# RWKV chunk inverses in compact 32 by 32 tiles on four row groups, with one off-diagonal block as the last level

## The chip, the cores and the metric

One core of a Trainium2 chip runs the whole kernel. The metric is the device time of one execution in microseconds (us). Five engines work side by side and wait for each other through semaphores: TensorE (matmuls, PE in the profile; its weight loads are PEld), VectorE (DVE), ScalarE (ACT), GpSimd (POOL) and SyncE (SP). Matmuls write PSUM, of which there are 8 banks; GpSimd does not read it here.

## The reference, cut to what matters

Two blocks of a transformer-like model on 256 tokens of width 1024, batch 1: feed-forward layers, attention, an RWKV-7 time mixing in layer 1, then a second block with convolution, dense and expert layers. The change touches only the RWKV recurrence, 16 heads of width 64:

```python
def rwkv7_step(state, inp):
    r_t, w_t, k_t, v_t, a_t, b_t = inp
    sa = jnp.einsum('bhvk,bhk->bhv', state, a_t)
    state = (state * w_t[:, :, None, :] + sa[..., None] * b_t[:, :, None, :]
             + v_t[..., None] * k_t[:, :, None, :])
    return state, jnp.einsum('bhvk,bhk->bhv', state, r_t)
```

## The kernel before, in words

The kernel does the recurrence in chunks of 64 tokens (C), 4 chunks for 256 tokens. Within a chunk the steps form a triangular system: the inverse of a 64 by 64 unit triangular matrix is wanted for each head and chunk, Ti and its transpose TiT. Two heads lie in one tile of 128 partitions, a *pair* (kt, 0 to 7); a pair has 4 chunks times 2 heads = 8 such matrices. In a tile of 128 by 256, half of the partitions (c = 0 or 1) hold the even or the odd chunk, and N_MAT = 4 matrices stand side by side.

The inverse starts from blocks of 2 by 2 and doubles the block with each *level*: LEVELS = (2, 4, 8, 16, 32). A level is two steps. In the first ("x"), TensorE multiplies the matrix masked to this level's off-diagonal blocks (lev, made by GpSimd, line 2073) with half the columns of Ti, and ScalarE copies the product to X (line 1944). In the second ("t"), TensorE multiplies X with half the columns of TiT and TiT with X, and VectorE adds both products to TiT (line 2010) and Ti (line 2013). The last level forms only TiT's product. After it, for each of the 4 chunks in turn, the step U multiplies TiT with the right sides, and S and keys carry the state on (n = 12 and later).

Before level 0 stand two steps: the scores ("sc", 64 columns of keys against rates), masked by VectorE (line 1986), and the scores of keys against rates once more, both ways round ("ab"), from which VectorE makes the first Ti and TiT (lines 1993, 1996, 1997). With level 1's x comes the product Xs, with levels 2 and 3 a transpose each of BH and KH (line 1869).

`rwkv_tensor` interleaves this by an order written out by hand. There are 4 rounds (UNITS); a round works on two pairs at once, pair 0 in `weights_hi_scratch` and banks 0 and 1, pair 1 in `weights_lo_scratch` and banks 2 and 3. A round has 25 steps; in each, TensorE takes one step of pair 0, one of pair 1, and then 1 to 9 128x128 products of 256 columns of the next round's projections (DENSE_STEPS; LAST_STEPS with the output projection in round 4). The other engines run the same steps in the same order: `pair_scalar`, `pair_vector` (with `finish_vector` of the pair before in it, whose first operation is a reciprocal, line 2053) and `pair_gpsimd`. TensorE's queue is in order: a step of pair 0 that waits holds pair 1 and the dense products behind it.

All these products are in f32 and each shows as two records of LDWEIGHTS and MATMUL. A product of 64 rows and 64 columns of weights takes one of the four 64x64 tiles of the array, by the partitions that it reads and writes. All matmuls but the transposes have line 428, a helper.

Of the kernel before, what the change touches and what calls it, by code (L numbers as in the profile page):

```python
# [13 lines left out]
P = 128  # L14
# [35 lines left out]
N_RW_MASK = 10  # L50
# [28 lines left out]
def constant_arrays():  # L79
# [36 lines left out]
    rw = [row6 < col6, row6 <= col6]  # L116
    for b in (1,) + LEVELS:
        rw.append((row6 // (2 * b) == col6 // (2 * b)) & (row6 % (2 * b) < b) & (col6 % (2 * b) >= b))
    rw += [rw[2].T, row6 == col6]
    rw = np.tile(np.concatenate(rw, axis=1).astype(np.float32), (2, 1))  # L120
# [1160 lines left out]
class RwkvTiles:  # L1281
    def __init__(self, k):
        A = KT * T
        self.ld, self.r, self.kx, self.a = (k.arena[:, i * A:(i + 1) * A] for i in range(4))
        self.g = k.arena[:, 5 * A:6 * A]
        self.xx = self.bonus = k.arena[:, 6 * A:7 * A]
        self.VN = k.arena[:, 10 * A:11 * A]
        self.xm = {MIX_W: self.VN, MIX_A: self.g, MIX_K: k.arena[:, 7 * A:8 * A], MIX_G: self.VN,
                   MIX_R: k.arena[:, 8 * A:9 * A], MIX_V: k.arena[:, 4 * A:5 * A]}
        at = 9 * A  # L1290
        self.lora = k.arena[:, at:at + 4 * T]
        at += 4 * T
# [5 lines left out]
        self.masks = k.arena[:, ARENA - N_RW_MASK * RW_CHUNK:ARENA]  # L1298
# [476 lines left out]
class PairTiles:  # L1775
# [8 lines left out]
    def __init__(self, k, t, kt, slot):  # L1784
# [6 lines left out]
        self.Ti, self.TiT, self.U = (first[:, at + i * N_MAT * C:at + (i + 1) * N_MAT * C] for i in range(3))  # L1791
        self.lev = [second[:, i * N_MAT * C:(i + 1) * N_MAT * C] for i in range(2)]
        self.KH, self.BH, self.Xs, self.y, self.y2 = (second[:, (2 + i) * T:(3 + i) * T] for i in range(5))
        self.VN = blk(t.VN, kt)
        self.X = [k.sq[:, (slot * 4 + i) * N_MAT * C:(slot * 4 + i + 1) * N_MAT * C] for i in range(4)]
        self.X.append(k.hidden_scratch[:, slot * N_MAT * C:(slot + 1) * N_MAT * C])
# [7 lines left out]
    def mask(self, i, n=1):  # L1804
        return self.masks[:, i * C:(i + n) * C].rearrange("p (o t) -> p o t", o=1).to_broadcast([P, N_MAT, n * C])
# [6 lines left out]
def mat(z, c, m):  # L1812

    return z[part(c), m * C:(m + 1) * C]

# [5 lines left out]
def pair_tensor(k, t, kt, slot):  # L1821
# [21 lines left out]
    for s in range(TT):  # L1843
        for h, c in QUADRANTS:
            ins = mm(k, mat(z.b[h], 1 - c, 2 + s), z.bt[part(h), chunk_columns(s, c)],
                     z.ar[part(h), 0, chunk_columns(s, c)], True, True)
    ins.then_inc(*p.step((kt, "ab")))
    yield
    for li, size in enumerate(LEVELS):
        last = li == len(LEVELS) - 1  # L1850
        pe.wait_ge(*d.at((kt, "t", li - 1)))
        pe.wait_ge(*g.at((kt, "level", li)))
        lev, X = z.lev[li % 2], z.X[li]
        for m in range(N_MAT):
            for c in range(2):
                ins = mm(k, dense(b0[part(1 - c), m * C // 2:(m + 1) * C // 2], size), mat(lev, c, m),
                         half_columns(mat(z.Ti, c, m), size, 0), True, True)
        ins.then_inc(*p.step((kt, "x", li)))
        if li == 1:
            pe.wait_ge(*k.rw_act.at(("turn", kt // PAIRS)))  # L1860
            for m in range(N_MAT):
                for c in range(2):
                    ins = mm(k, mat(b1, 1 - c, m), z.MakT[part(c), m // 2 + m % 2 * 2, :], mat(z.VN, c, m), True, True)
# [13 lines left out]
        for m in range(N_MAT):  # L1877
            for c in range(2):
                ins = mm(k, dense(b1[part(c), m * C // 2:(m + 1) * C // 2], size), mat(X, c, m),
                         half_columns(mat(z.TiT, c, m), size, 1), True, True)  # L1880
            if not last:
                for c in range(2):
                    ins = mm(k, dense(b0[part(1 - c), m * C // 2:(m + 1) * C // 2], size), mat(z.TiT, c, m),
                             half_columns(mat(X, c, m), size, 0), True, True)
        ins.then_inc(*p.step((kt, "t", li)))
        yield
    for n in range(4):
        s, c = divmod(n, 2)
        if n > 0:
            pe.wait_ge(*(a.at((kt, "S", 1)) if n == 1 else d.at((kt, "S", n))))  # L1890
            for h in range(2):
                ins = mm(k, z.b[h][part(1 - c), P:P + HEAD], z.ar[part(h), 0, chunk_columns(s, c)], z.S[n][part(h), :],
                         True, True)
# [3 lines left out]
        else:  # L1897
            pe.wait_ge(*d.at((kt, "tt", len(LEVELS) - 1)))
        for h in range(2):
            ins = mm(k, b1[part(c), h * HEAD:(h + 1) * HEAD], mat(z.TiT, 1 - c, 2 * h + s), mat(z.Xs, 1 - c, 2 * s + h),  # L1900
# [33 lines left out]
def pair_scalar(k, t, kt, slot):  # L1934
# [7 lines left out]
    for li, size in enumerate(LEVELS):  # L1942
        act.wait_ge(*p.at((kt, "x", li)))
        act.copy(half_columns(z.X[li], size, 0), dense(b0[:, 0:N_MAT * C // 2], size)).then_inc(*a.step((kt, "X", li)))
# [29 lines left out]
def pair_vector(k, t, kt, slot):  # L1974
# [8 lines left out]
    for h in range(2):  # L1983
# [3 lines left out]
                          z.b[h][:, :].rearrange("p (m x) -> p m x", m=N_MAT), z.mask(0, 2), ALU.mult)\  # L1987
# [3 lines left out]
    for h in range(2):  # L1991
        for to, at, mask in ((z.Ti, 0, 8), (z.TiT, P, 2)):
            dve.tensor_tensor(mats(to)[:, 2 * h:2 * h + 2, :], z.b[h][:, at:at + P].rearrange("p (m t) -> p m t", m=2),
                              z.mask(mask)[:, 0:2, :], ALU.mult).then_inc(*d.step((kt, "T0", h, mask)))
    dve.wait_ge(*d.at((kt, "T0", 1, 2)))
    dve.tensor_tensor(mats(z.Ti), mats(z.Ti), z.mask(9), ALU.add).then_inc(*d.step((kt, "t", -1)))
    dve.tensor_tensor(mats(z.TiT), mats(z.TiT), z.mask(9), ALU.add).then_inc(*d.step((kt, "TiT")))
    yield
    earlier = finish_vector(k, t, kt - PAIRS, slot) if kt >= PAIRS else None
    for li, size in enumerate(LEVELS):  # L2000
# [8 lines left out]
        piece = half_columns(z.TiT, size, 1)  # L2009
        dve.tensor_tensor(piece, piece, dense(b1[:, 0:N_MAT * C // 2], size), ALU.add).then_inc(*d.step((kt, "tt", li)))  # L2010
        if not last:
            piece = half_columns(z.Ti, size, 0)
            dve.tensor_tensor(piece, piece, dense(b0[:, 0:N_MAT * C // 2], size), ALU.add)\
                .then_inc(*d.step((kt, "t", li)))
        yield
    for n in range(4):
        s, c = divmod(n, 2)
        if n > 0:
# [3 lines left out]
            for h in range(2):  # L2022
                piece = mat(z.Xs, 1 - c, 2 * s + h)
                ins = dve.tensor_tensor(piece, z.b[h][part(1 - c), P:P + HEAD], piece, ALU.add)
# [43 lines left out]
def pair_gpsimd(k, t, kt, slot):  # L2068
# [3 lines left out]
    def level(li):  # L2072
        pool.tensor_tensor(mats(z.lev[li % 2]), z.MabT, z.mask(3 + li), ALU.mult).then_inc(*g.step((kt, "level", li)))
# [6 lines left out]
    pool.wait_ge(*d.at((kt, "sc", 1)))  # L2080
# [3 lines left out]
    pool.wait_ge(*p.at((kt, "ab")))  # L2084
# [3 lines left out]
    for li in range(len(LEVELS) - 2):  # L2088
        pool.wait_ge(*p.at((kt, "x", li)))
        level(li + 2)  # L2090
        yield

# [1137 lines left out]
```

## Time and profile before

| | |
|---|---|
| time, median of 3 runs | 2735.32 us (2733.24 to 2735.78) |
| the profiled execution | 2738.52 us, span 2737.0 us, mean granted TensorE clock 0.985 |
| busy over the span: TensorE, its weight loads, VectorE, ScalarE, GpSimd | 96%, 84%, 76%, 59%, 8% |
| the four RWKV rounds | 785 to about 1010 us of the span |

The span runs from the first to the last instruction; the time of the execution is 1.5 us more. Matmuls are pipelined and their ends are modelled, so a busy TensorE need not be one at its peak, and the starts of its records tell more than their lengths. A granted clock of 1.00 is 2.4 GHz, 0.50 is 1.2 GHz.

### The profile page before, as it was taken

The page shows a single profiled execution, that of the slowest core. Times are in us where ns is not written, and L with a number is a line of the kernel's source. Part 1 is how long each engine was busy: PE and PEld are TensorE (multiplying, and loading weights), DVE is VectorE, ACT ScalarE, POOL GpSimd, SP SyncE. Part 2 cuts the span into 40 slices and gives each one's busy share as a digit, 9 for nine tenths or more (in the row PEclk, how much of TensorE's full clock was granted, in tenths as well). Part 3 has the DMA queues.
Part 4 walks back from the last instruction along what each step waited for, and adds up shares of the span by engine and source line. Part 5 has one row for each costly group of instructions (what it writes and reads, how often), then busy time and mean ns, then how long its engine had stood idle before and what let it go on. Part 6 is the DMA issues. An engine that isn't in the chain of part 4 may idle for free.

```text
span 2737.0 us, 43598 instructions
## 1 busy us (share of the span) xinstructions
PE 2635.5 (96%) x17668; PEld 2290.9 (84%) x17668; DVE 2068.2 (76%) x2973; ACT 1614.9 (59%) x2394; POOL 226.1 (8%) x229
## 2 busy tenths in 40 slices
PE   8999899999899999999999898999999999999997
PEld 7989789899787779998899896888888888888886
DVE  6667776776744557668655686999999999999995
ACT  5556455555332235543555535877787778778785
POOL 1102000000011117011600010000000000000000
PEclk9999999999999999999999999999999999999999
DMA  7553245455331125543355433999999999899992
GB/s 272 185 185 110 106 169 185 172 183 185 113 106 67 66 92 185 185 166 116 135 186 185 145 130 122 378 351 349 352 375 351 349 351 366 335 364 363 352 375 82
DMA packets 84605, 604.91 MB, mean 221 GB/s; under 512 B 9400, under 2 KB 9528, under 8 KB 12016
## 3 DMA queue, kind: packets, MB, share of 16 engines
q1 hardware_dynamic: 82016, 594.05, 58.9%
q10 hardware_dynamic: 2032, 4.85, 0.5%
q8 instruction: 144, 2.36, 0.4%
q0 software_dynamic: 352, 3.15, 0.3%
q14 instruction: 61, 0.50, 0.1%
HBM read 600.96 MB, written 1.05 MB: 220 GB/s over the span
## 4 chain that ended last, share of the span: by engine, by line
PE 88%; DVE 9%; ACT 2%; issue 1%; DMA 1%; ACTq 0%; DVEq 0%
PE bank L428 86%; DVE arena L2266 2%; DVE weights_lo L418 2%; PE bank L2856 1%; DVE arena L1200 1%; ACT weights_hi L410 1%; DVE rstd L479 1%; DMA x_T<-in_x 0%; DVE x_T L734 0%; DVE arena L2289 0%; DVE arena L555 0%; DVE arena L1202 0%; ACT x_T L546 0%; DVE arena L2980 0%; PE bank L1869 0%
## 5 line engine op out<-in xcount | busy, mean ns | idle before, releaser
L418 DVE TENSOR_TENSOR weights_lo<-raw_weights,weights_hi 128x1024 fp32r<-128x1024 f32 x816 | 1004.1, 1249 | 389.5 <-ACT weights_hi L410 383.9
L410 ACT CAST weights_hi<-raw_weights 128x1024 fp32r<-128x1024 f32 x816 | 849.5, 1050 | 333.4 <-PE bank L428 319.1
L428 PE MATMUL bank<-source,weights_hi 128*128 128x512 f32 (+1 forms) x3040 | 876.7, 356 | 43.0 <-DVE weights_lo L418 18.2
L428 PE MATMUL bank<-source,weights_lo 128*128 128x256 f32 x2400 | 682.2, 284 | 0.0
L428 PEld LDWEIGHTS bank<-source,weights_hi 128*128 128x128 f32 x3040 | 541.8, 194 | 130.6 <-issue 28.0
L428 PEld LDWEIGHTS bank<-source,weights_lo 128*128 128x128 f32 x2400 | 463.2, 193 | 0.1
L418 DVE TENSOR_TENSOR weights_lo<-arena,weights_hi 128x1024 fp32r<-128x1024 f32 x278 | 336.5, 1225 | 32.0 <-ACT weights_hi L410 28.5
L410 ACT CAST weights_hi<-arena 128x1024 fp32r<-128x1024 f32 x278 | 292.2, 1053 | 56.5 <-PE bank L428 40.3
L428 PE MATMUL bank<-weights_hi,source 128*128 128x512 f32 (+1 forms) x1024 | 309.6, 386 | 3.4 <-issue 2.8
L428 PE MATMUL bank<-hidden_hi,weights_hi 128*128 128x256 f32 x912 | 258.3, 283 | 0.0
L428 PE MATMUL bank<-hidden_lo,weights_hi 128*128 128x256 f32 x912 | 258.1, 283 | 0.0
L428 PE MATMUL bank<-hidden_hi,weights_lo 128*128 128x256 f32 x912 | 257.9, 283 | 0.0
L428 PEld LDWEIGHTS bank<-weights_hi,source 128*128 128x128 f32 x1024 | 186.3, 191 | 36.7 <-issue 4.1
L428 PE MATMUL bank<-weights_lo,source 128*128 128x512 f32 (+1 forms) x512 | 195.0, 381 | 0.0
L428 PE MATMUL bank<-weights_hi,hidden_hi 128*128 128x512 f32 x448 | 174.9, 390 | 6.2 <-issue 4.1
L428 PE MATMUL bank<-weights_hi,other_source_hi 128*128 128x512 f32 x448 | 179.7, 401 | 0.0
L428 PEld LDWEIGHTS bank<-hidden_hi,weights_hi 128*128 128x128 f32 x912 | 174.7, 192 | 2.6
L428 PE MATMUL bank<-weights_lo,other_source_hi 128*128 128x512 f32 x448 | 175.2, 391 | 0.0
L428 PEld LDWEIGHTS bank<-hidden_hi,weights_lo 128*128 128x128 f32 x912 | 174.9, 192 | 0.0
L428 PEld LDWEIGHTS bank<-hidden_lo,weights_hi 128*128 128x128 f32 x912 | 174.8, 192 | 0.1
L428 PE MATMUL bank<-weights_hi,other_source_lo 128*128 128x512 f32 x448 | 174.7, 390 | 0.0
L428 PE MATMUL bank<-weights_lo,hidden_hi 128*128 128x512 f32 x448 | 174.4, 389 | 0.0
(317 smaller groups left out, 3387.0 us busy)
## 6 DMA issues: line engine op xcount, KB each, us to landing
raw_weights<-in_exp_in SPq DMA_DIRECT2D x134, 1024.0 KB, 5.4
arena<-in_exp_in SPq DMA_DIRECT2D x90, 1024.0 KB, 5.4
raw_weights<-in_exp_w SPq DMA_DIRECT2D x67, 1024.0 KB, 5.3
arena<-in_exp_w SPq DMA_DIRECT2D x45, 1024.0 KB, 5.6
raw_weights<-in_ffn_w_down SPq DMA_DIRECT2D x44, 1024.0 KB, 5.0
raw_weights<-in_ffn_w_up SPq DMA_DIRECT2D x43, 1024.0 KB, 5.0
raw_weights<-in_ffn_w_gate SPq DMA_DIRECT2D x42, 1024.0 KB, 4.9
raw_weights<-in_dense_w SPq DMA_DIRECT2D x33, 1024.0 KB, 4.9
```

The costliest lines, as they stand in the source:

```text
L410: k.act.copy(k.weights(j)[0], raw_half(k, j)).then_inc(k.w_hi_ready, 1)
L418: k.dve.tensor_tensor(lo, raw_half(k, j), hi.bitcast(F32), ALU.subtract).then_inc(k.w_ready, 1)
L428: return k.pe.matmul(dst, lhsT, rhs, start=start, stop=stop, skip_group_check=shared)
L479: k.dve.reciprocal(k.rstd[:, :], k.std[:, :]).then_inc(*k.normed.step((f, "rstd")))
L1200: k.dve.reciprocal(s_r, s_s).then_inc(*k.at_dve.step(("root", u)))
L2266: ins = k.dve.scalar_tensor_tensor(y, tap, w, y, ALU.mult, ALU.add)
L2856: ins = k.pe.transpose(bank[:, i * P:(i + 1) * P], k.act_buf[:, n % 2 * T + i * P:n % 2 * T + (i + 1) * P], ident)
```

## The change

Up to blocks of 32, Ti, TiT, the level masks and X are kept as 32 by 32 blocks: of each 64 by 64 matrix only the two diagonal blocks (b = 0, 1). Partitions 32 (2c + b) and on hold block b of chunk parity c, and the tiles are 128 by 128 where they were 128 by 256. The products of levels 0 to 3 are then 32 by 32, each on the diagonal tile of one of four row groups, with 16 streamed columns where there were 32, and twice as many. The ab step gives the blocks directly: 32 columns of weights, 32 streamed, twice as many products. The last level is one block: the masked product (`MabT`) of rows 0 to 31 and columns 32 to 63 with Ti's first block, copied by ScalarE to X32, times TiT's second block; VectorE copies the result to its place in `full`, a 64 by 64 form of TiT, whose diagonal blocks GpSimd copies from TiT once level 3 is done. U reads `full`. VectorE first copies the ab scores to M, from which GpSimd makes the level masks (before: from MabT) and VectorE the first TiT. Xs and the state products keep their chunk's partition half, where they wrote the other. The masks are smaller. The core of the diff, VectorE's and GpSimd's parts after TensorE's:

```diff
-    for s in range(TT):
-        for h, c in QUADRANTS:
-            if s == 0 and c == h:
-                pe.wait_ge(*d.at((kt, "sc", h)))
-            mm(k, mat(z.b[h], c, s), z.ar[part(h), 0, chunk_columns(s, c)], z.bt[part(h), chunk_columns(s, c)],
-               True, True)
...
+    for turned in range(2):
+        for s in range(TT):
+            for b in range(2):
+                for h, c in QUADRANTS:
...
+                    keys, rates = z.bt[part(h), block_columns(s, c, b)], z.ar[part(h), 0, block_columns(s, c, b)]
+                    lhsT, rhs = (keys, rates) if turned else (rates, keys)
+                    ins = mm(k, tile32(z.b[h], c, b, 2 * turned + s), lhsT, rhs, True, True)
...
+        if last:
+            for m in range(N_MAT):
+                for c in range(2):
+                    ins = mm(k, tile32(b0, c, 1, m), z.MabT[rows32(c, 0), m, BLOCK:C], tile32(z.Ti, c, 0, m), True, True)
+        else:
...
+            for m in range(N_MAT):
+                for c in range(2):
+                    for b in range(2):
+                        ins = mm(k, half_tile(b0, c, b, m, size), tile32(lev, c, b, m),
+                                 half_columns(tile32(z.Ti, c, b, m), size, 0), True, True)
...
         for m in range(N_MAT):
+            if last:
+                for c in range(2):
+                    ins = mm(k, tile32(b1, c, 0, m), tile32(z.X32, c, 1, m), tile32(z.TiT, c, 1, m), True, True)
+                continue
             for c in range(2):
-                ins = mm(k, dense(b1[part(c), m * C // 2:(m + 1) * C // 2], size), mat(X, c, m),
-                         half_columns(mat(z.TiT, c, m), size, 1), True, True)
-            if not last:
-                for c in range(2):
-                    ins = mm(k, dense(b0[part(1 - c), m * C // 2:(m + 1) * C // 2], size), mat(z.TiT, c, m),
-                             half_columns(mat(X, c, m), size, 0), True, True)
+                for b in range(2):
+                    ins = mm(k, half_tile(b1, c, b, m, size), tile32(X, c, b, m),
+                             half_columns(tile32(z.TiT, c, b, m), size, 1), True, True)
+            for c in range(2):
+                for b in range(2):
+                    ins = mm(k, half_tile(b0, c, b, m, size), tile32(z.TiT, c, b, m),
+                             half_columns(tile32(X, c, b, m), size, 0), True, True)
...
             pe.wait_ge(*d.at((kt, "tt", len(LEVELS) - 1)))
+            pe.wait_ge(*g.at((kt, "full")))
...
     for h in range(2):
-        for to, at, mask in ((z.Ti, 0, 8), (z.TiT, P, 2)):
-            dve.tensor_tensor(mats(to)[:, 2 * h:2 * h + 2, :], z.b[h][:, at:at + P].rearrange("p (m t) -> p m t", m=2),
-                              z.mask(mask)[:, 0:2, :], ALU.mult).then_inc(*d.step((kt, "T0", h, mask)))
-    dve.wait_ge(*d.at((kt, "T0", 1, 2)))
-    dve.tensor_tensor(mats(z.Ti), mats(z.Ti), z.mask(9), ALU.add).then_inc(*d.step((kt, "t", -1)))
-    dve.tensor_tensor(mats(z.TiT), mats(z.TiT), z.mask(9), ALU.add).then_inc(*d.step((kt, "TiT")))
+        ins = dve.tensor_copy(z.M[:, 2 * h * BLOCK:2 * (h + 1) * BLOCK], z.b[h][:, 2 * BLOCK:4 * BLOCK])
+    ins.then_inc(*d.step((kt, "M")))
+    for h in range(2):
+        dve.tensor_tensor(mats(z.Ti)[:, 2 * h:2 * h + 2, :],
+                          z.b[h][:, 0:2 * BLOCK].rearrange("p (m t) -> p m t", m=2),
+                          z.mask(5, 2), ALU.mult).then_inc(*d.step((kt, "T0", h)))
+    dve.wait_ge(*d.at((kt, "M")))
+    dve.tensor_tensor(mats(z.TiT), mats(z.M), z.mask(0), ALU.mult).then_inc(*d.step((kt, "TiT0")))
+    dve.wait_ge(*d.at((kt, "TiT0")))
+    dve.tensor_tensor(mats(z.Ti), mats(z.Ti), z.mask(6), ALU.add).then_inc(*d.step((kt, "t", -1)))
+    dve.tensor_tensor(mats(z.TiT), mats(z.TiT), z.mask(6), ALU.add).then_inc(*d.step((kt, "TiT")))
...
+    pool.wait_ge(*d.at((kt, "tt", len(LEVELS) - 2)))
+    for c in range(2):
+        for b in range(2):
+            ins = pool.tensor_copy(mats(z.full)[rows32(c, b), :, b * BLOCK:(b + 1) * BLOCK], mats(z.TiT)[rows32(c, b), :, :])
+    ins.then_inc(*g.step((kt, "full")))
```

The helpers that it calls:

```python
def rows32(c, b):
    return slice((2 * c + b) * BLOCK, (2 * c + b + 1) * BLOCK)

def tile32(z, c, b, m):
    return z[rows32(c, b), m * BLOCK:(m + 1) * BLOCK]

def half_tile(bank, c, b, m, size):
    return dense(bank[rows32(c, b), m * BLOCK // 2:(m + 1) * BLOCK // 2], size)
```

## Rows read from the trace of the kernel before

**Rows 1.** The page, part 4: the chain that ended last, by engine and by line.

```profile
...
PE 88%; DVE 9%; ACT 2%; issue 1%; DMA 1%; ACTq 0%; DVEq 0%
PE bank L428 86%; DVE arena L2266 2%; DVE weights_lo L418 2%; PE bank L2856 1%; DVE arena L1200 1%; ACT weights_hi L410 1%; DVE rstd L479 1%; DMA x_T<-in_x 0%; DVE x_T L734 0%; DVE arena L2289 0%; DVE arena L555 0%; DVE arena L1202 0%; ACT x_T L546 0%; DVE arena L2980 0%; PE bank L1869 0%
...
```

**Rows 2.** Busy time by stretch: us from:to, its length, then busy us (instructions) by engine.

```profile
...
785.00:954.00 169.00, 167.73 (x2888) 133.59 (x2892) 80.40 (x239) 39.31 (x118) 29.93 (x42) 1.00 0.18 64
954.00:1010.00 56.00, 54.46 (x912) 42.68 (x904) 27.53 (x73) 10.72 (x35) 10.12 (x14) 0.91 0.20 77
785.00:1010.00 225.00, 222.20 (x3788) 176.27 (x3789) 107.93 (x312) 50.03 (x152) 40.05 (x56) 0.98 0.19 68
...
```

**Rows 3.** The waits between 785 and 1010 us: total us, times, longest.

```profile
...
PEld bank L428 <- DVE weights_lo_scratch L1996: 1.6, 1, 1.6
...
PE bank L428 <- DVE weights_hi_scratch L2013: 1.1, 2, 0.5
...
```

**Rows 4.** Timeline, TensorE, round 1: start us, us until the last ends, what, xrecords.

```profile
...
789.03 1.16 PE L428 MATMUL bank<-arena 64*64 64x64 f32 x64
790.12 1.13 PE L428 MATMUL bank<-normed_T,consts 128*128 128x256 f32 x4
...
791.52 1.46 PE L428 MATMUL bank<-arena,raw_weights 128*128 128x256 f32 x6
792.91 0.66 PE L428 MATMUL bank<-weights_hi_scratch 64*64 64x32 f32 x16
793.56 0.66 PE L428 MATMUL bank<-weights_lo_scratch 64*64 64x32 f32 x16
...
795.20 0.25 PE L428 MATMUL bank<-weights_hi_scratch,squares 64*64 64x32 f32 x2
795.22 0.25 PE L428 MATMUL bank<-squares,weights_hi_scratch 64*64 64x32 f32 x2
795.28 0.23 PE L428 MATMUL bank<-weights_hi_scratch,squares 64*64 64x32 f32 x2
...
795.69 0.23 PE L428 MATMUL bank<-weights_lo_scratch,squares 64*64 64x32 f32 x2
...
```

**Rows 5.** Timeline, TensorE, round 1: a product with 2 streamed columns.

```profile
...
823.62 1.05 PE L428 MATMUL bank<-consts,normed_T 128*128 128x2 f32 x8
824.54 0.68 PE L428 MATMUL bank<-arena,raw_weights 128*128 128x256 f32 x2
```

**Rows 6.** Timeline, VectorE, round 3: both pairs, from the first mask.

```profile
...
904.03 0.88 DVE L1993 TENSOR_TENSOR weights_hi_scratch<-bank,arena 128x128 f32<-128x128 f32 x4 [0.85 <-PE bank L428]
...
907.65 0.41 DVE L1997 TENSOR_TENSOR weights_lo_scratch<-weights_lo_scratch,arena 128x256 f32<-128x256 f32 x1
...
```

**Rows 7.** Groups by form, the rounds: busy us, mean ns of one, idle before.

```profile
...
L2024 DVE TENSOR_TENSOR weights_hi_scratch<-bank,weights_hi_scratch 64x64 f32<-64x64 f32 x24 | 4.2, 215 | 22.9 <-PE bank L428 22.9
...
L2073 POOL TENSOR_TENSOR weights_hi_scratch<-weights_hi_scratch,arena 128x256 f32<-128x256 f32 x20 | 15.3, 766 | 200.9 <-DVE weights_hi_scratch L1986 174.7 <-PE bank L428 26.2
...
L2351 POOL MEMSET arena<- 128x64 f32 x6 | 0.6, 150 | 179.4 <-DVE x_T L2439 179.4
...
```

**Rows 8.** Timeline, TensorE, round 3, levels 0 and 1.

```profile
...
907.78 0.66 PE L428 MATMUL bank<-weights_lo_scratch 64*64 64x32 f32 x16
...
911.72 0.66 PE L428 MATMUL bank<-weights_hi_scratch 64*64 64x32 f32 x16 [0.54 <-DVE weights_hi_scratch L2013]
...
913.74 1.13 PE L428 MATMUL bank<-arena,raw_weights 128*128 128x256 f32 x4
...
```

**Rows 9.** Timeline, TensorE, round 4, levels 0 and 1.

```profile
...
961.16 1.01 PE L428 MATMUL bank<-weights_lo_scratch 64*64 64x32 f32 x16 [1.54 <-DVE weights_lo_scratch L1996]
...
970.73 1.49 PE L428 MATMUL bank<-arena,raw_weights 128*128 128x256 f32 x4
...
```

**Rows 10.** Timeline, VectorE and TensorE, round 4: level 3, first U.

```profile
...
982.29 0.29 DVE L2010 TENSOR_TENSOR weights_lo_scratch<-weights_lo_scratch,bank 128x128 f32<-128x128 f32 x1
...
986.57 0.44 PE L428 MATMUL bank<-weights_hi_scratch 64*64 64x64 f32 x4
...
```

More of the change, by code:

```diff
@@ L49 @@
 LEVELS = (2, 4, 8, 16, 32)
-N_RW_MASK = 10
+BLOCK = 32
+N_SMALL_MASK = 7
+RW_MASKS = 2 * RW_CHUNK + N_SMALL_MASK * BLOCK
 PARAMS = [
@@ L115, in constant_arrays @@
     row6, col6 = row[0:RW_CHUNK], col[:, 0:RW_CHUNK]
[L116 to L120, printed above, removed]
+    wide = np.tile(np.concatenate([row6 < col6, row6 <= col6], axis=1).astype(np.float32), (P // RW_CHUNK, 1))
+    row3, col3 = row[0:BLOCK], col[:, 0:BLOCK]
+    small = []
+    for b in (1,) + LEVELS[:-1]:
+        small.append((row3 // (2 * b) == col3 // (2 * b)) & (row3 % (2 * b) < b) & (col3 % (2 * b) >= b))
+    small += [small[0].T, row3 == col3]
+    rw = np.concatenate([wide, np.tile(np.concatenate(small, axis=1).astype(np.float32), (P // BLOCK, 1))], axis=1)
     t = np.arange(T)
@@ L1851, in pair_tensor @@
         pe.wait_ge(*d.at((kt, "t", li - 1)))
-        pe.wait_ge(*g.at((kt, "level", li)))
-        lev, X = z.lev[li % 2], z.X[li]
-        for m in range(N_MAT):
-            for c in range(2):
-                ins = mm(k, dense(b0[part(1 - c), m * C // 2:(m + 1) * C // 2], size), mat(lev, c, m),
-                         half_columns(mat(z.Ti, c, m), size, 0), True, True)
+        if last:
[3 more added lines that the diff above has]
+        else:
+            pe.wait_ge(*g.at((kt, "level", li)))
+            lev, X = z.lev[li % 2], z.X[li]
+            for m in range(N_MAT):
[3 more added lines that the diff above has]
+                                 half_columns(tile32(z.Ti, c, b, m), size, 0), True, True)
         ins.then_inc(*p.step((kt, "x", li)))
@@ L1943, in pair_scalar @@
         act.wait_ge(*p.at((kt, "x", li)))
-        act.copy(half_columns(z.X[li], size, 0), dense(b0[:, 0:N_MAT * C // 2], size)).then_inc(*a.step((kt, "X", li)))
+        if li == len(LEVELS) - 1:
+            ins = act.copy(z.X32, b0[:, 0:N_MAT * BLOCK])
+        else:
+            ins = act.copy(half_columns(z.X[li], size, 0), dense(b0[:, 0:N_MAT * BLOCK // 2], size))
+        ins.then_inc(*a.step((kt, "X", li)))
         if 0 < li < 4:
@@ L2008, in pair_vector @@
             dve.wait_ge(*d.at((kt, "TiT")))
-        piece = half_columns(z.TiT, size, 1)
-        dve.tensor_tensor(piece, piece, dense(b1[:, 0:N_MAT * C // 2], size), ALU.add).then_inc(*d.step((kt, "tt", li)))
-        if not last:
+        if last:
+            for c in range(2):
+                ins = dve.tensor_copy(mats(z.full)[rows32(c, 0), :, BLOCK:C],
+                                      b1[rows32(c, 0), 0:N_MAT * BLOCK].rearrange("p (m t) -> p m t", m=N_MAT))
+            ins.then_inc(*d.step((kt, "tt", li)))
+        else:
+            piece = half_columns(z.TiT, size, 1)
+            dve.tensor_tensor(piece, piece, dense(b1[:, 0:N_MAT * BLOCK // 2], size), ALU.add)\
+                .then_inc(*d.step((kt, "tt", li)))
             piece = half_columns(z.Ti, size, 0)
-            dve.tensor_tensor(piece, piece, dense(b0[:, 0:N_MAT * C // 2], size), ALU.add)\
+            dve.tensor_tensor(piece, piece, dense(b0[:, 0:N_MAT * BLOCK // 2], size), ALU.add)\
                 .then_inc(*d.step((kt, "t", li)))
@@ L2072, in level @@
     def level(li):
-        pool.tensor_tensor(mats(z.lev[li % 2]), z.MabT, z.mask(3 + li), ALU.mult).then_inc(*g.step((kt, "level", li)))
+        pool.tensor_tensor(mats(z.lev[li % 2]), mats(z.M), z.mask(1 + li), ALU.mult).then_inc(*g.step((kt, "level", li)))
     def hat(src, name):
@@ L2087, in pair_gpsimd @@
     hat(z.kt_, "KH")
-    for li in range(len(LEVELS) - 2):
+    for li in range(len(LEVELS) - 3):
         pool.wait_ge(*p.at((kt, "x", li)))
```

45 lines of the change are left out of this document (25 added, 20 removed).

## The prediction

> **What bounds the kernel now.** I read the page first: the chain that ended last is 88% TensorE, 86% of it line 428, which every matmul shares [rows 1]. The change touches only the four RWKV rounds, 785 to 1010 us, so I asked for those windows next: TensorE is busy 222.20 of 225 us, VectorE 107.93, ScalarE 50.03, GpSimd 40.05 [rows 2]. A busy TensorE may only be pipelined, so two checks. The waits list gives it few waits on other engines: 1.6 us once for line 1996, 1.1 us in two waits for line 2013 [rows 3]. And the timeline shows matmul groups starting back to back [rows 4]. So TensorE's own spacing of matmuls sets the time here; a nanosecond off it comes off the span, except where it merely reaches a wait sooner.
>
> **The unit: a slot.** A product in f32 is two records. Records on one tile of the array follow each other in fixed slots; different tiles run side by side. In the t products of level 0, records of four 64x64 tiles start together (795.20, 795.22), the next four from 795.28, and pair 1's begin at 795.69: seven groups in 0.41 us, so 58.4 ns a slot, 0.49 us for the 8 slots of a pair with the longer first one (80 ns) [rows 4]. 64 columns streamed cost no more: 64 such records take 1.09 us to the next group, 16 slots again. The stream is thus not what fills the slot. With 128 columns of weights and 2 streamed columns a record takes 0.92/8 = 115 ns, its first one long as well [rows 5]. Half the weight columns, half the slot: loading the weights sets it, 50 to 57 ns per 64 columns. For 32 columns I extrapolate (58.4 - 50/2) to (58.4 - 57/2) = 30 to 33 and take 32 ns. Bounds: 29 ns (half of 58.4) and 58.4 (it does not shrink).
> On this price alone a page can be asked: the Trainium skill, "TensorE: Matmul & The Clock Gate", section LDWEIGHTS, has the load cost its columns at 1.2 GHz whatever the rows, 27 ns for 32. By it, as an estimate, the slots below would come to 120 x 27 = 3.2 us a pair; no trace here has a 32-column load.
>
> **Slots per pair (8 pairs).** Now: the second group of scores ("ab", 32 records on 4 tiles) 8; X products of levels 0 to 3 (16 records on 2 tiles) 8 each; their t products (32 on 4) 8 each; the last level's two phases 8 each: 8 + 32 + 32 + 16 = 88 x 58.4 = 5.14 us. After: ab has 64 records on 8 tiles, 8 slots; X has 32 records on the 4 diagonal tiles, 8; t has 64 on the same 4, 16; the last level is 8 products in each of two phases, on 2 tiles, 8 and 8: 8 + 32 + 64 + 16 = 120 x 32 = 3.84 us. Eight pairs: **-10.4 us**. The break-even slot is 5140/120 = 42.8 ns; the bounds give -13.3 (29 ns) and +15.0 (58.4).
>
> **Tile size switches.** Six 128-row records start at 791.52 and the next 64x64 group at 792.91: 1.39 us where 6 x 0.216 is 1.30. Back again, 789.03 to 790.12 is 1.09 where 16 slots are 0.94 to the last start plus 0.06 [rows 4]. A change of tile size costs 0.09 us each way. Most steps keep their count, since dense work already stands between them. New is level 1: X (32x32), Xs (64x64), X, Xs adds 3 switches a round, 12 in all, 1.1 us, and 0.3 for the long first slots behind them: **+1.4 us**. No row has 32x32 against 64x64; bounds 0 and, at twice the price, 2.8.
>
> **VectorE at a round's start.** Before TensorE's second X group, VectorE masks four PSUM pieces per pair (0.22 us apart) and makes two 128x256 products with masks: 904.03 to 908.06 for both pairs, 4.0 us [rows 6]. After: two copies and two masks of half the width from PSUM, one mask and two adds at 128x128. A 64x64 PSUM operation still takes 0.215 [rows 7], so little is saved on each: 4 x 0.18 + 3 x 0.25 = 1.46 a pair, 2.9 for both, 1.1 less; with ab ending 0.2 earlier for pair 0, VectorE is 1.3 ahead. What waits on it:
> - Rounds 1 to 3, pair 1's first X: 793.56 comes 0.65 after 792.91 where 0.49 is enough. **-0.15 x 3**, gone.
> - Rounds 2 and 3, level 1: TensorE idle 0.54 before 911.72 behind line 2013 [rows 8]. TensorE comes 0.9 sooner (0.42 ab, 0.42 X, 0.15, less 0.09 t), VectorE 1.4: 0.5 of the 0.54 goes. **-0.47 x 2**. The two reciprocals of the previous pairs, 3.3 us between, stay and are late next.
> - Round 4, pair 1's first X: idle 1.54 before 961.16 [rows 9]. VectorE 1.06 sooner for that operand, TensorE 0.63: **-0.43**.
> Together -1.8; bounds 0 and -3.3, all of these waits.
>
> **Costed at nothing.** ScalarE's copies of X halve in width and have 1.0 us of dense work behind them. GpSimd's level masks go from 128x256 (0.77 us) to 128x128, one fewer per pair; level 0's now waits for the VectorE copy M, the first thing VectorE does after ab, and has over 2 us until its X. The mask load is smaller. New on GpSimd: four copies per pair of the diagonal blocks into the full matrix, behind level 3's VectorE add (line 2010, 982.29), before U (986.57, pair 1's 0.29 later) [rows 10]. GpSimd does nothing else then; behind them in its queue stands only the next round. With the last level 0.84 shorter, 8 copies have 3.7 us. Bounds for one: 0.15 (memset 128x64) and 0.77 (128x256 product) [rows 7]; at 0.3 they take 2.4 and hide; at 0.77 pair 1's U waits 2.5 a round. After the rounds, TensorE goes straight on into the output projection, and the DMA engines are busy 0.20 of round 4 [rows 2], so the gain is not given back to a transfer.
>
> **Sum.** -10.4 + 1.4 - 1.8 = -10.8 us. The profiled execution took 2738.5 (span 2737.0), 3.2 above the median of 2735.3. In it the granted clock fell from 2.4 to 1.2 GHz in round 4 right behind the 1.54 us idle. From pair 1's first X to the dense work behind Xs took 9.57 us there (961.16 to 970.73) against 5.95 in round 3 (907.78 to 913.74) [rows 8, 9]: 3.6 us, about what the profile lies above the median. So 2735.3 - 10.8 = 2724.5, or, if the shorter idle spares the fall, 2738.5 - 10.8 - 3.6 = 2724.1. I say **2724**.
>
> **A rule against it.** Four tiles' records start within 0.02 us and 32 of them within 0.49 us, 15 ns each [rows 4]. The change adds 112 products a pair, 1792 records in all, each streaming only 16 columns. The Trainium skill, "TensorEngine Tiling (Array Packing)", section Instruction Overhead, holds that every matmul carries some 60 cycles however few its columns, and advises against taking tiles from a dimension already small. Were that a price for the whole engine (25 ns), the added records alone would cost an estimated +45 us; the rows refute this, as a floor per tile it lies under my 32 ns.
>
> **Rivals.**
> 1. *The small records cost the same slot or arrive no faster.* 58.4 ns for 32 columns gives +15.0 + 1.4 - 1.8 = +14.6, **2750**. The same sign if the engine takes one record per 15 ns, the densest long run seen: t and ab then need 64 x 15 = 0.96 against 0.49, +0.47 x 40 = +18.8, less 0.4: 2754. It is slower from a mean slot of about 43 ns. For: no 32-column load in the trace, nothing denser than 15 ns for long. Against: 115 to 58 on halving the columns, and groups of four within 0.02 us.
> 2. *A slot half way*, about 40 ns: 120 x 40 = 4.8, -2.7 - 0.4 = -3.1, **2732**.
> 3. *The clock.* Smaller tiles occupy less of the array; round 4 shows the clock fall after idling, the first three rounds hold 1.00 [rows 2]. If every round's levels fell, 4 x 3.6 = 14.4 on top of -10.8: +3.6, **2739**. Against: dense work at full width stands in every step.
> 4. *The full matrix comes late*: 2.5 us in rounds 2 to 4 (round 1 has more dense work there), 7.5, **2732**.
>
> **Chances and range.** Forecast 68% (2718 to 2730, by a slot of 29 to 35 ns, switches of nothing to 1.4, waits of 0 to -3.3), rival 1 13%, rival 2 8%, rival 3 6%, rival 4 5%. One measurement tells 0.2%, 5.5 us. Faster: the forecast and about half of rivals 2 and 4, 0.74; slower: rival 1 and half of rival 3, 0.17; the rest 0.09. The range, 2717 to 2741, takes in all but rival 1 and scraps.
>
> **What would show it.** In the profile after: LDWEIGHTS of 32 columns with starts on one tile 32 ns apart; t of a pair in 0.51 us (now 0.49), X in 0.27; 12 more switches of 0.09; line 428's records up by 1792; no wait of TensorE for GpSimd's copies; the rounds some 11 us shorter and the clock at 1.00 in rounds 1 to 3. A t phase near 1 us, or TensorE waiting for the full matrix, would prove me wrong.

## The result, and the profile after

2793.5 us, the median of 4 runs (2784.0 to 2804.3), against 2734.3 before (also 4 runs now): ratio **1.0215 [1.0189, 1.0242]**, 59 us slower. The forecast was 2724, with a range of 2717 to 2741. The profiled execution took 2788.6 (span 2787.0), 50.1 more than that of before, and the whole of it lies in the rounds: TensorE's first score record to the first product behind the rounds now takes 285.6 us, where it took 234.2.

The page after: TensorE's count, what released the chain, and the queue that brings instructions.

```profile
span 2787.0 us, 47222 instructions
PE 2673.1 (96%) x19460; PEld 2314.3 (83%) x19460; DVE 2066.4 (74%) x2989; ACT 1613.1 (58%) x2394; POOL 218.3 (8%) x253
...
q8 instruction: 158, 2.59, 0.4%
...
PE 88%; DVE 8%; ACT 2%; issue 1%; DMA 1%; ACTq 0%; DVEq 0%
```

The records are up by 1792 (17668 before), as forecast. The instruction queue has 14 packets more than before's 144: 1792 loads and 1792 matmuls are 14 times 256 instructions. The chain of waits looks as in [rows 1]; its shares tell nothing. The stretches tell it; columns as in [rows 2]. Rounds 1 to 4, each cut where the levels end, then all of it:

```profile
786.77:827.80 41.03, 38.30 (x1139) 30.20 (x1139) 11.68 (x41) 7.52 (x22) 8.73 (x20) 0.83 0.14 54
827.80:854.75 26.95, 26.95 (x290) 21.20 (x286) 11.33 (x38) 5.95 (x19) 0.00 (x0) 1.00 0.23 79
854.75:893.15 38.40, 35.09 (x1115) 26.99 (x1114) 17.15 (x50) 6.56 (x20) 8.19 (x20) 0.75 0.17 59
893.15:926.70 33.55, 33.55 (x282) 25.19 (x278) 11.21 (x37) 5.53 (x18) 0.00 (x0) 0.72 0.08 32
926.70:963.80 37.10, 34.74 (x1116) 26.78 (x1115) 17.02 (x49) 6.55 (x20) 8.19 (x20) 0.77 0.17 61
963.80:989.27 25.47, 25.43 (x283) 19.75 (x279) 11.42 (x38) 5.50 (x18) 0.00 (x0) 1.00 0.12 43
989.27:1028.20 38.93, 31.20 (x1105) 24.15 (x1104) 15.23 (x44) 5.55 (x18) 8.22 (x20) 0.82 0.29 112
1028.20:1072.30 44.10, 42.80 (x308) 31.93 (x304) 19.12 (x47) 12.20 (x28) 0.00 (x0) 0.73 0.13 47
786.77:1072.30 285.53, 268.06 (x5616) 206.19 (x5616) 114.16 (x341) 55.37 (x163) 33.33 (x80) 0.81 0.17 61
```

Two things are new. First, the granted clock: 0.81 over the rounds, where [rows 2] had 0.98. The same steps, of rounds 2 and 3, took 33.55 us at 0.72 and 25.47 at 1.00. A granted clock of 0.72 means that 56% of the stretch, 18.8 us, ran at 1.2 GHz, and these cost 8.1 us: **0.43 us for each us at 1.2 GHz**. Second, TensorE is idle: busy 31.20 of 38.93 us in round 4's levels. Its waits in the rounds (us in all, times, longest), beside [rows 3]:

```profile
PE bank L432 <- issue: 12.1, 13, 2.5
PE bank L1903 <- issue: 3.0, 2, 1.5
...
PE bank L432 <- DVE weights_lo_scratch L2045: 1.1, 1, 1.1
```

"issue" is a wait for nothing that the profile shows: **15.1 us in 15 holes**, of which the rounds had none before. They open in the middle of a step's products. Three that follow each other in round 4 (timeline), and the records between them (stretches):

```profile
1015.79 0.20 PE L432 MATMUL bank<-weights_lo_scratch,squares 32*32 32x16 f32 x2 [0.35 <-issue]
1019.75 0.44 PE L1903 MATMUL bank<-consts,arena 128*128 128x128 f32 x2 [1.54 <-issue]
1023.42 0.25 PE L432 MATMUL bank<-squares,weights_lo_scratch 32*32 32x16 f32 x7 [1.20 <-issue]
```

```profile
1015.80:1019.70 3.90, 2.41 (x127) 1.75 (x127) 1.02 (x4) 0.80 (x3) 0.00 (x0) 1.00 0.02 4
1019.70:1023.40 3.70, 2.48 (x127) 2.00 (x127) 0.35 (x2) 0.37 (x1) 1.14 (x4) 1.00 0.02 4
```

127 loads, 127 matmuls and two waits are 256 instructions, one packet of 16 KB of the instruction queue, and the holes are 3.7 and 4.0 us apart at full clock. The other holes of the rounds stand whole multiples of 256 instructions apart too, to one instruction, with TensorE's waits counted in. My reading: TensorE's program comes in instruction pages of 256, and the next one was not there.

### The profile page after: what moved, and what is told of

It reads as the page before. It is cut to its first block, busy times and chain, and to the rows that moved or that the text cites. A ratio compares the mean times of both kernels' runs of the same rounds, so it can differ in the third digit from the quotient of the medians.

```text
span 2787.0 us, 47222 instructions
## 1 busy us (share of the span) xinstructions
PE 2673.1 (96%) x19460; PEld 2314.3 (83%) x19460; DVE 2066.4 (74%) x2989; ACT 1613.1 (58%) x2394; POOL 218.3 (8%) x253
## 4 chain that ended last, share of the span: by engine, by line
PE 88%; DVE 8%; ACT 2%; issue 1%; DMA 1%; ACTq 0%; DVEq 0%
PE bank L432 86%; DVE arena L2326 2%; DVE weights_lo L422 2%; PE bank L2916 1%; DVE arena L1204 1%; ACT weights_hi L414 1%; DVE rstd L483 1%; PE bank L1903 0%; DMA x_T<-in_x 0%; DVE x_T L738 0%; DVE arena L2349 0%; DVE arena L559 0%; DVE arena L1206 0%; ACT x_T L550 0%; DVE arena L3040 0%
## 5 line engine op out<-in xcount | busy, mean ns | idle before, releaser
L432 PE MATMUL bank<-arena,raw_weights 128*128 128x256 f32 (+2 forms) x624 | 185.2, 439 | 8.7 <-DVE arena L1699 8.7
```

The costliest lines, as they stand in the source:

```text
L432: return k.pe.matmul(dst, lhsT, rhs, start=start, stop=stop, skip_group_check=shared)
```

## The experiments

Medians, each beside before's on the same chip, and the ratio with its 95% interval; "rounds" is the length of the rounds in the profiled execution, with its clock there, "issue" the sum of TensorE's waits of that name in the rounds (for supply alone, in the added products).

The recorded texts below name three explanations. Theory A: the program is supplied too slowly, which makes the holes, and the holes let the clock fall. Rival B: there is no such limit, and the holes belong to the 32x32 tiles. Rival C: small tiles lower the clock by themselves.

| kernel | us | before | ratio | rounds, clock | issue |
|---|---|---|---|---|---|
| after | 2793.5 | 2734.3 | 1.0215 [1.0189, 1.0242] | 285.6, 0.81 | 15.1 |
| 64x64 products doubled | 2760.8 | 2736.3 | 1.0103 [1.0085, 1.0120] | 258.9, 0.99 | 5.6 |
| half of the products | 2747.9 | 2736.3 | 1.0042 [1.0009, 1.0075] | 244.0, 0.90 | 0.4 |
| more dense work | 2772.7 | 2736.3 | 1.0135 [1.0119, 1.0152] | 272.7, 0.99 | 6.5 |
| last block alone | 2732.6 | 2736.3 | 0.9982 [0.9971, 0.9993] | 230.0, 0.99 | 0 |
| supply alone | 2825.7 | 2736.5 | one run | | 29.2 |
| dense work earlier | 2786.7 | 2736.5 | 1.0189 [1.0173, 1.0204] | 284.5, 0.84 | 17.0 |
| half, round 4 covered | 2745.8 | 2736.5 | 1.0042 [1.0027, 1.0057] | 223.9, 0.99 | 0 |
| last block, round 4 covered | 2729.3 | 2736.5 | 0.9975 [0.9963, 0.9987] | 227.8, 1.00 | 0 |
| small filler | 2839.4 | 2733.4 | 1.0388 [1.0365, 1.0412] | 327.1, 0.75 | 5.7 |
| idle | 2845.0 | 2733.4 | 1.0397 [1.0370, 1.0424] | 341.1, 0.71 | 33.6 |
| cover alone | 2733.3 | 2733.4 | 0.9997 [0.9986, 1.0007] | 230.2, 1.00 | 0 |
| half the idle | 2771.1 | 2735.3 | 1.0117 [1.0073, 1.0161] | 275.5, 0.87 | 14.0 |

**Supply alone.**

```diff
+    for i in range(1024):
+        r = slice(i % 4 * 32, i % 4 * 32 + 32)
+        mm(k, k.bank[0][r, 0:16], ident[r, 0:32], ident[r, 0:16], True, True)
+    for i in range(512):
+        r, q = slice(i % 2 * 64, i % 2 * 64 + 64), slice(i // 2 % 2 * 64, i // 2 % 2 * 64 + 64)
+        mm(k, k.bank[i % 2][q, 0:16], ident[r, 0:64], ident[r, 0:16], True, True)
     for p in range(UNITS):
```

> The kernel before with 1024 products of 32x32 on four diagonal tiles (2048 records) and 512 of 64x64 on the four 64x64 tiles (1024 records) in a row ahead of the first round, with operands in SBUF and no waits. Theory A (the program comes in pages of 256 instructions, one per 3.4 to 4 us when none is in stock): after the stock is used up both sections run at the same pace of 27 to 31 ns a record, whatever the tile: 55 to 64 us for the first section (16 pages), 27 to 32 us for the second (8 pages); holes end at multiples of 256 instructions; the whole 2817 to 2831. Rival B (no limit of supply; the tiles' own pace of 8 ns a record for 32x32, 14.6 ns for 64x64): 17 and 15 us, no holes, 2767.

A stretch of the first section, and the instruction queue in it (packets, MB, share):

```profile
785.50:837.70 52.20, 26.60 (x1792) 25.10 (x1793) 0.00 (x0) 0.00 (x0) 0.00 (x0) 0.50 0.02 6
```

```profile
q8 instruction: 14, 0.23, 1.8%
```

```profile
785.50 1.90 PE L428 MATMUL bank<-consts 32*32 32x16 f32 x128 [2.51 <-issue]
788.96 1.90 PE L428 MATMUL bank<-consts 32*32 32x16 f32 x128 [1.55 <-issue]
```

128 records run in 1.9 us, then TensorE stands; 1792 records and 14 packets in 52.2 us, **3.73 us for 256 instructions, 29.1 ns a record**, with no work on the other engines. The whole section is at 1.2 GHz (clock 0.50), and yet the pace is that of the changed kernel's holes at full clock, 3.7 to 4.0 us. A limit of supply by itself is thus shown, and 2825.7, a single run, lies in its range. The 64x64 section ran at 28.8 ns, but at 1.2 GHz its own pace is about that (two times 14.6), so it tells nothing. In the section "Instruction fetch mechanics" of the page "Runtime: NRT & Kernel Launch", the Trainium skill has the same blocks of 256 instructions, fetched one while another runs; it holds that the fetch is hidden behind the issue of instructions. The blocks agree with the 256 between holes; the hiding does not hold here, and the measurement decides.

**64x64 products doubled.**

```diff
-            for c in range(2):
+            for c in (0, 1) if last else (0, 1, 0, 1):
                 ins = mm(k, dense(b1[part(c), m * C // 2:(m + 1) * C // 2], size), mat(X, c, m),
...
+                if li != 1:
+                    mm(k, dense(b1[part(c), m * C // 2:(m + 1) * C // 2], size), mat(lev, c, m),
+                       half_columns(mat(z.Ti, c, m), size, 0), True, True)
```

> The kernel before with its 64x64 products doubled, until its levels issue as many matmul records as the changed kernel's (112 more products a pair but for 8, 104): each ab product and each t product of levels 0 to 3 is issued twice, and each X product of levels 0, 2, 3 and 4 once more on one of the two idle tiles. By slots of 58.4 ns the added work costs 8 slots in 32 t steps and 8 in 8 ab steps, 15.0 + 3.7 = +18.7 us, and nothing for X: 2753. Theory A (TensorE's program arrives in pages of 16 KB, 256 instructions, and no faster than one in 3.4 to 4 us; the levels of the changed kernel use them up faster): holes in the middle of groups at 256-instruction boundaries here as well, 10 to 20 us in all, 2763 to 2775, more if the clock falls behind them. Rival B (the holes are a matter of the 32x32 tiles): no holes, 2753. Rival C (the clock falls because tiles are small, not because of holes): granted clock of the rounds 0.98 as before, whether or not there are holes.

```profile
PE bank L428 <- issue: 5.6, 8, 1.8
```

Holes without a single 32x32 tile: rival B falls. They are 5.6 us, less than the 10 to 20 expected (2753 + 5.6 is 2759, measured 2760.8). That the doubled work takes longer and so leaves the supply more time is my explanation, not tried. The clock held (0.99), as rival C had it: 5.6 us of holes among 64x64 products, twice as many as before, did not lower it.

**Half of the products.**

```diff
-                    for b in range(2):
+                    for b in range(1):
                         ins = mm(k, half_tile(b0, c, b, m, size), tile32(lev, c, b, m),
```

> The changed kernel with the products of the second diagonal block (b = 1) left out in ab and in the X and t steps of levels 0 to 3: as few instructions as before, 8 slots for X and 16 for t on each tile that still works, half of the tiles idle. What is left out makes the result another one; the time is what counts. By slots the time is the changed kernel's forecast, 2724. Theory A: no holes, and since the holes' idle lets the clock fall, a clock near 0.98 in the rounds, 2720 to 2732. Rival B (32x32 tiles make the holes): holes stay, 2740 or more. Rival C (small tiles lower the clock by themselves): no holes, but a granted clock of 0.85 or less in the rounds, 2750 to 2775.

Its rounds 2 and 4:

```profile
841.17:893.32 52.15, 51.41 (x945) 40.27 (x944) 28.40 (x86) 12.01 (x38) 8.62 (x20) 1.00 0.19 63
...
946.10:1027.10 81.00, 78.52 (x961) 59.00 (x960) 34.09 (x91) 17.70 (x46) 8.28 (x20) 0.68 0.20 77
```

As many instructions as before, and the holes are gone (0.4 us of issue in all). Round 2 takes 52.15 us, where it took 53.96 before: with a clock of 1.00 and no holes, these small products, half as many, save time. But the clock fell without holes: 0.90 in the rounds, median 2748, between the ranges of theory A and of rival C and nearer C's. Theory A's second half, that the holes make it fall, is refuted in this form. The clock fell behind round 4's wait for VectorE, so I took that for the trigger.

**Half, with round 4's wait covered.**

```diff
-LAST_STEPS = [2, 2] + [2, 1] * 5 + [1] * 10 + [2, 2, 1]
+LAST_STEPS = [2, 4] + [2, 1] * 5 + [1] * 10 + [1, 1, 1]
```

> The changed kernel with the products of the second diagonal block left out as before (its output is another one), and in round 4 two dense products moved from the last steps to behind ab, where TensorE idled for VectorE and the clock fell for 51 us (2747). If the idle starts the fall and the small work only keeps the clock from coming back: no fall in round 4 in most runs, clock 0.985 or more, 2718 to 2726. If small tiles lower the clock by themselves: the fall stays, at 0.975 to 0.98, 2742 to 2748.

2745.8, as without it: the first branch is wrong, and the time and the clock (0.974 to 0.980 in all runs but one) are those of the second, small tiles by themselves. The profiled run, 2722.6, is the exception: no fall in round 4 and rounds of 223.9 us, 10.4 less than before; the other seven took 2739 to 2756. The idle of round 4 was not what decides.

**More dense work, and the same filler on a small tile.**

```diff
         pe.wait_ge(*d.at((kt, "t", li - 1)))
+        if li > 0:
+            mm(k, b1[:, 2 * P:4 * P], ident, k.const[:, 0:2 * P], True, True)
...
+        mm(k, b0[:, 2 * P:4 * P], ident, k.const[:, 0:2 * P], True, True)
```

> The changed kernel with one more 128x128 product of 256 columns (constants times constants, into columns that nobody reads) ahead of the small products of each X step from level 1 on and of each t step: 9 a pair, 72 in all, 2 records of 0.216 us each, and for the second pair of a round two tile size switches of 0.09: +38 us by its own work. If holes and the fallen clock are what the change costs, the denser work thins out the instructions per us and keeps the clock up: 2724 + 38 = 2762, so faster than the changed kernel's 2793 by some 30 us although it does more; granted clock of the rounds 0.95 or more, holes under 8 us. If both have another cause (a wait, the products themselves): 2793 + 38 = 2831.

In the second kernel these products read `ident[0:32, 0:32]` and `k.const[0:32, 0:2 * P]`.

> The changed kernel with the same 72 additional products as in the run with more dense work, but on one 32x32 tile instead of the whole array (32 rows and 32 columns of weights, 256 streamed columns, the same 0.216 us a record, no tile size switch): 72 x 0.43 = 31 us of TensorE time that thins out the instructions as before but leaves the array nearly empty. If the holes alone let the clock fall (theory A): holes as few as there (4 to 6 us), clock 0.985, 2724 + 4 + 31 + 5 = 2764. If work on few rows and columns lowers the clock by itself (rival C): the same few holes, but a clock of 0.965 or less, 2785 to 2815.

With 128x128 filler:

```profile
786.73:1059.41 272.68, 264.35 (x5760) 203.89 (x5761) 114.25 (x341) 55.09 (x164) 33.09 (x80) 0.99 0.18 63
...
PE bank L432 <- issue: 6.5, 5, 2.7
```

With 32x32 filler:

```profile
785.69:1112.76 327.07, 319.73 (x5761) 231.73 (x5761) 114.44 (x341) 55.33 (x164) 32.78 (x80) 0.75 0.15 52
...
PE bank L432 <- issue: 5.7, 8, 1.9
```

The changed kernel with 72 products more is **21 us faster** than without them. Both fillers take as many instructions and leave as few holes (6.5 and 5.7 us); only how much of the array they fill differs. With full width the clock is 0.99, with 32 by 32 it is 0.75, and 67 us lie between them. Neither time was forecast well: 2772.7 for 2762, and 2839.4 is 24 us above even rival C's range. The kernel with the small filler was at 1.2 GHz for 54.6 us on end in round 2. The 3.0 us before, and that stretch:

```profile
869.90:872.90 3.00, 2.77 (x113) 1.97 (x106) 2.48 (x8) 0.18 (x1) 0.36 (x2) 1.00 0.03 5
872.90:927.50 54.60, 54.60 (x791) 36.09 (x788) 9.49 (x39) 6.51 (x23) 3.07 (x10) 0.50 0.07 22
```

TensorE had been busy for 2.77 of 3.00 us. Narrow work lowers the clock with hardly any idle, and no more than its twin has: rival C is right in this.

**Idle in the kernel before**, and half as much.

```diff
         for m in range(N_MAT):
+            if m == 2 and not last and kt % PAIRS == 0:
+                for _ in range(48):
+                    pe.wait_ge(*k.rw_pre_dve.at(("ops", kt // PAIRS)))
```

> The kernel before with idle time in the middle of pair 0's t step in levels 0 to 3 of each round: a row of waits that are long met, 24 or more of 51 ns each, 1.2 us or more, 16 times: about as much idle as the holes of the changed kernel, in the same steps, but with 64x64 tiles. If idle of this size in the levels lets the clock fall (theory A): the time grows by the idle (20 us) and by a fallen clock, 0.975 or less, 2775 or more. If the tiles decide (rival C): clock 0.98 to 0.987, 2735 + 20 = 2755.

```profile
786.99:1128.04 341.05, 304.59 (x3825) 234.86 (x3825) 116.33 (x325) 57.01 (x164) 39.57 (x56) 0.71 0.14 50
```

> The kernel before with half the row of met waits in the same 16 places: by the run with the whole row (48 waits, holes of 2.3 us) holes of 1.2 us, 18 to 19 us in all, which is the sum of the holes of the changed kernel, on 64x64 tiles. If idle alone of this size is what lowers the changed kernel's clock: clock 0.965 to 0.970, 2735 + 18.5 + some 35 = 2785 to 2795. If the narrow tiles have to come with it: clock 0.98 or more, 2752 to 2762. Between them, both count.

```profile
787.53:1063.07 275.54, 258.65 (x3825) 202.14 (x3825) 115.92 (x325) 56.99 (x164) 39.52 (x56) 0.87 0.18 62
...
PE bank L428 <- issue: 14.0, 16, 1.1
```

The first idle came out larger than meant, 33.6 us; with it the clock fell to 0.71 on unchanged 64x64 tiles. The second gave 14.0 us of the 18.5 expected, about the changed kernel's holes: two of four runs took 2758 to 2760 (clock of the whole run 0.98) and two 2782 (0.97). So idle alone lowers the clock too, and narrow tiles do; the changed kernel has both. At its median this kernel loses 36 us, 14 as idle and some 22 by the clock, where the changed kernel loses 42 by the clock (worked out below): an estimate of the share that idle alone has, and a rough one, since the four runs fall into two groups.

**Dense work earlier.** (LAST_STEPS likewise, for round 4.)

```diff
-DENSE_STEPS = [4, 5] + [2, 1] * 5 + [2] * 10 + [3, 3, 2]
+DENSE_STEPS = [4, 5] + [2, 2] * 5 + [2, 1] * 5 + [3, 3, 2]
```

> The changed kernel with 5 of each round's dense products moved from the later steps into the level steps, nothing added: rounds 1 to 3 [2, 2] instead of [2, 1] a level and [2, 1] instead of [2, 2] behind them, round 4 likewise. Theory A: five levels get 2.1 us more cover, so holes shrink by about as much a round (some 6 of the 15 us), and the levels are denser in 128-row work, so the clock falls less often: 2765 to 2785. If only waits of the later steps come of it: 2793 to 2800.

Missed: 2786.7, just above the range; issue is 17.0 us, not less, and the clock 0.84 for 0.81. Five products a round, moved, are too few; the 18 above, added, held the clock and left 6.5 us of issue.

**The parts that could stay.** The last level alone (its first phase; the rest of the edit is the change's):

```diff
+        if last:
+            for m in range(N_MAT):
+                for c in range(2):
+                    ins = mm(k, b0[rows32(1 - c, 1), m * 32:(m + 1) * 32], z.MabT[rows32(c, 0), m, 32:C],
+                             half_of(z.Ti, c, 0, m, 0), True, True)
```

> The kernel before with one part of the change alone: the last level as one off-diagonal block of 32x32 products in the old 64x64 layout, with ScalarE's copy of it in compact form, two VectorE copies of 32x128 in the place of one 128x128 add, and no GpSimd mask for that level. As many records as before. By slots: 16 of 58.4 ns become 16 of 32 ns a pair, 0.42 us, 8 pairs: -3.4 us; VectorE's second copy may take 0.15 of it back a round. All theories: no new holes, 2731 (2729 to 2734). Rival C, that small products lower the clock by themselves, would show a clock fall behind level 4 in most rounds and 2735 to 2745.

with the covered wait of round 4 (the edit of LAST_STEPS above):

> The kernel before with the last level as one block of 32x32 products, and in round 4 two dense products moved from the last steps to behind ab, ahead of pair 1's first X, where TensorE is idle for 1.54 us. The block gives -3.4 (2731); the cover takes 0.86 of the idle, and if that idle is what starts the fall of the clock in round 4, the 3.6 us of the fall go too: 2727 (2725 to 2729). If the clock falls all the same: 2730 to 2731.

and that cover alone:

> The kernel before with the moved dense products of round 4 alone (two of them from the last steps to behind ab), to split the 7 us that this and the last block gained together: block 3.4 by slots, so 3.6 from the cover, of which 0.86 is the idle and the rest the clock: 2731 to 2733. If the gain was the block's alone: 2735 to 2736.

The block gave 3.7 us for the forecast's 3.4 (the interval allows 2 to 8), and the clock held. Together with the cover it is 2729.3, just above the 2725 to 2729 expected, and **0.9975 [0.9963, 0.9987]**: the version that beats both kernels. The cover alone measured 2733.3 against 2733.4, so the 3.6 us expected of it are not there, though its profiled run has no fall in round 4; whether it adds anything to the block is inside the uncertainty.

## Why the prediction was wrong

**Two steps failed.** The sum, -10.4 + 1.4 - 1.8, has no term for a fall of the clock that the small products bring: it leaves the rounds at the clock of before, and rival 3 gave a fall 6%, 3.6 us a round and only the levels. That was the larger error, +42 us. And the step "TensorE's own spacing of matmuls sets the time here", true of the kernel before, was carried over to twice as dense a program: +15 us. I had checked waits and tiles, but not how fast the program itself arrives. The trace of before has no such hole in the rounds, so the pace of supply was not in it; the demand was. In level 1 of its round 2:

```profile
865.00:869.00 4.00, 4.00 (x105) 3.07 (x104) 1.62 (x6) 0.90 (x3) 0.00 (x0) 1.00 0.19 45
```

That is 38 ns a record (a load and a matmul), above the 29 of the supply. The change adds 96 records to a level of both pairs and takes a little time away: about 20 ns a record, below it.

The 51.3 us more in the rounds, by the profiled runs:
- *Rival 3, the clock: mechanism named, size wrong.* I gave it 6% and 3.6 us a round, 14.4. By the clock of each stretch above, 107 us are at 1.2 GHz; before, 10 (0.91 of the 56 us in [rows 2]). The 97 more cost, at 0.43, **+42**. The price is that of the chunk steps, taken for the levels too. Other kernels, by the length and clock of their rounds, give 0.39 (idle, its issue taken off), 0.44 (half the idle) and 0.45 (half of the products, without and with the cover), so it is good to some 4 us. The falls last, into the chunk steps behind the levels (0.72 in round 2), where I had priced the levels alone. "Dense work at full width stands in every step" was no protection.
- *Instruction supply: in no rival.* **+15.1**.
- *The products themselves, with switches and waits*: what is left, **-6**, where -10.8 was forecast. The terms below, read from steps without holes at full clock, add up to about the same. No kernel ran that has all of the small products and neither holes nor falls, so this is worked out, not measured whole. The one with more dense work comes nearest: its 272.7 us less 6.5 of issue, 2 for the clock and the 38 of its added work (an estimate) are some 226, where before without its fall has 230: -4.

Its terms. *X: right*, -6.7 us in all. After, round 1, both pairs' X and t to the next product, and round 3, ab:

```profile
795.06 0.44 PE L432 MATMUL bank<-weights_hi_scratch 32*32 32x16 f32 x32
795.34 0.45 PE L432 MATMUL bank<-weights_lo_scratch 32*32 32x16 f32 x32
...
796.78 0.25 PE L432 MATMUL bank<-weights_hi_scratch,squares 32*32 32x16 f32 x8
...
798.02 0.70 PE L432 MATMUL bank<-arena,raw_weights 128*128 128x256 f32 x2
...
930.54 1.32 PE L432 MATMUL bank<-arena 64*32 64x32 f32 x128
931.78 0.92 PE L432 MATMUL bank<-normed_T,consts 128*128 128x256 f32 x3
```

The same t with half of its products, 64 records instead of 128:

```profile
850.15 0.24 PE L432 MATMUL bank<-weights_hi_scratch,squares 32*32 32x16 f32 x4
...
851.27 0.70 PE L432 MATMUL bank<-arena,raw_weights 128*128 128x256 f32 x2
```

X of a pair takes 0.28 us (forecast 0.27). The half t takes 1.12, just the 32 slots of 32 ns and a switch of 0.09 that the slot model has.

*t and ab: mis-sized.* The full t has the same slots on each tile and takes 1.24, and ab, of the 16 slots of 32 ns that I gave it on its eight tiles, takes 1.24 as well. What they share is 128 records: less the switch, **9 ns a record** for the whole engine, a floor beside the slots. X, 32 records in 0.28, has that pace too, so it fits both prices. The floor is rival 1's second form, at 9 and not 15 ns. Against before, t comes out +0.17 a step (1.07 before), 16 steps, +2.8 (forecast +1.4), ab +0.15 a round against 1.09 [rows 4], +0.6 (forecast -1.7).

*Switches and waits: as forecast as far as seen.* The step of level 1 with Xs in it takes 1.96 us for 2.01, which is the -0.42 of X and three switches; the wait for VectorE in round 4 is 1.1 us for 1.5, and the two of 0.5 are gone.

*The partition half: costed at nothing*, since the diff only turns `part(1 - c)` into `part(c)`. The last U (c = 1) before read `TiT` in half 0 and wrote half 1, a tile that the 16 records of y_states beside it leave free. Now it reads and writes half 1, the tile of the eight y_states records of the second head (h = 1). From its first record to the next dense one, before (round 2) and after (round 1):

```profile
890.66 0.27 PE L428 MATMUL bank<-weights_hi_scratch 64*64 64x64 f32 x1
...
891.75 0.48 PE L428 MATMUL bank<-arena,raw_weights 128*128 128x256 f32 x1
```

```profile
845.54 0.27 PE L432 MATMUL bank<-weights_hi_scratch,hidden_hi_scratch 64*64 64x64 f32 x1
...
847.08 1.13 PE L432 MATMUL bank<-arena,raw_weights 128*128 128x256 f32 x4
```

1.09 against 1.54 us: 4 records a pair, 8 slots of 58 ns for both, +0.45 a round. At full clock every kernel with the new layout shows 1.54 and every one with the old 1.09; that the shared tile is the cause is read from this and from the order of the records, not tried by itself. I had counted slots per step, but not whose tile they take.

*GpSimd's full copies*: no wait for them, as forecast.

**Right as well**: the last level (3.7 measured alone, 3.4 forecast), 1792 records. **The range** ended at 2741, just above rival 3's 2739, and left rival 1 out; but even the worst case in the text, 2754, is 40 us below the result. Nothing in it let two limits that both depend on the number and width of instructions go wrong together.

Open: what decides in which round the clock falls. Runs of one kernel differ (the half kernel with cover 2723 to 2756), and only profiled ones show where. In the one of the changed kernel, each of the six falls in the rounds begins in a hole or within 1.1 us behind one, and nine holes have none. Around the 1.5 us hole of round 2:

```profile
871.00:874.00 3.00, 1.45 (x76) 0.99 (x73) 1.50 (x6) 0.00 (x0) 0.00 (x0) 1.00 0.02 5
874.00:877.00 3.00, 3.00 (x69) 2.41 (x70) 0.00 (x0) 1.17 (x4) 0.00 (x0) 0.52 0.02 5
```

So here idle seems to say where a fall begins. It isn't needed: the small filler's fall above had 0.2 us of it. How the two act together is not shown.

## What to carry to other kernels

Before splitting products into more and smaller ones, count TensorE's instructions over the densest few us and compare with the 256 per 3.7 us measured here; slots saved are lost again if the program can't arrive. Read the granted clock by stage, and price a fall by how long it lasts. When operands change their partitions, list for each step which tile each product takes.

## What the runs showed of the hardware

- TensorE's program arrives in instruction pages of 256, 3.73 us each when it waits for them (29 ns a record of load and matmul), at either clock; holes stand 256 instructions or a multiple apart and are named "issue".
- 128 records of 32x32 on four tiles and 128 of 64x32 on eight take the same 1.24 us, 9 ns a record less the switch; 64 of 32x32 on two tiles take 1.12, 32 ns a slot.
- Work on 32 rows and columns in the place of the same time at 128 by 128 took the clock of the rounds from 0.99 to 0.75; 33.6 us of idle in 16 pieces took it to 0.71 from 0.98 on unchanged 64x64 tiles.
- 0.43 us is lost per us at 1.2 GHz in the chunk steps, 0.39 to 0.45 by the rounds of other kernels.
